# A two-layer encoder trunk in split-fp32 matmuls: the FFN in three parts, and the matmul operands moved to the front of SBUF

## The reference, cut to what matters

```python
for layer in range(2):
    h = rms_norm(x, mixer_norm_w[layer])
    if layer == 0:   # banded attention beside spatial gating, from ONE projection of 3584 columns
        mixed = concatenate([attn, sgu]) @ hyb_w_out
    else:            # stick-breaking attention, 16 heads of 128
        mixed = attention(h @ sb_w_qkv) @ sb_w_out
    x = x + mixed
    h = rms_norm(x, ffn_norm_w[layer])
    x = x + (silu(h @ w_gate[layer]) * (h @ w_up[layer])) @ w_down[layer]   # hidden width 5632
```

## Time and profile before

| what | value |
|---|---|
| median of the runs | 2164.94 us |
| the profiled execution, span | 2163.0 us |
| TensorE busy | 2156.0 us (100%) |
| VectorE busy | 1178.2 us (54%) |
| ScalarE busy | 988.2 us (46%) |
| read from HBM | 395.62 MB, mean 184 GB/s |
| granted TensorE clock in the slices | 9 tenths or more in all 40 |

### The profile page before, as it was taken

The page is one execution under the profiler, slowest core; times in us unless marked ns, Lnnn a source line. Parts: engine busy times, 40 slices in busy tenths (PEclk is TensorE's granted clock), DMA queues, the critical chain, the costliest instruction groups (busy, mean ns, idle before and its releaser), DMA issues.

```text
span 2163.0 us, 26223 instructions
## 1 busy us (share of the span) xinstructions
PE 2156.0 (100%) x9708; PEld 1769.2 (82%) x9708; DVE 1178.2 (54%) x1282; ACT 988.2 (46%) x1150; POOL 8.8 (0%) x19
## 2 busy tenths in 40 slices
PE   9999999999999999999999999999999999999999
PEld 8777888888888888888888888888888888888887
DVE  6777555555555544444565566555555555544443
ACT  6466554444444444444455445554444444443433
POOL 1000000000000000000000000000000000000000
PEclk9999999999999999999999999999999999999999
DMA  9544565565556545555545554556555655555553
GB/s 327 184 137 156 175 194 187 183 193 186 190 187 194 190 166 186 177 203 185 191 159 162 169 174 159 177 189 194 186 184 192 194 185 185 192 175 190 199 203 107
DMA packets 199154, 398.41 MB, mean 184 GB/s; under 512 B 6641, under 2 KB 6657, under 8 KB 198849
## 3 DMA queue, kind: packets, MB, share of 16 engines
q1 hardware_dynamic: 197728, 392.72, 55.3%
q0 software_dynamic: 960, 2.90, 0.4%
q10 hardware_dynamic: 416, 2.13, 0.3%
HBM read 395.62 MB, written 2.10 MB: 184 GB/s over the span
## 4 chain that ended last, share of the span: by engine, by line
PE 98%; ACT 1%; DVE 1%; DMA 0%; issue 0%; SPq 0%
PE acc L956 31%; PE acc L958 31%; PE acc L957 31%; PE turn L972 2%; PE turn L1042 0%; PE turn L1092 0%; PE zb L1067 0%; DVE w_lo L622 0%; PE zb L1027 0%; DMA raw<-in_w_in 0%; PE turn L1010 0%; PE zb L1068 0%; PE turn L1093 0%; ACT w_hi L418 0%; ACT att L526 0%; PE zb L1080 0%
## 5 line engine op out<-in xcount | busy, mean ns | idle before, releaser
L622 DVE TENSOR_TENSOR w_lo<-raw,w_hi 128x1024 fp32r<-128x1024 f32 (+1 forms) x760 | 906.6, 1201 | 697.5 <-ACT w_hi L418 696.2
L418 ACT ACTIVATE w_hi<-raw 128x1024 fp32r<-128x1024 f32 (+1 forms) x760 | 790.7, 1041 | 929.5 <-PE acc L958 926.3
L956 PE MATMUL acc<-w_hi,xT_hi 128*128 128x512 f32 x2016 | 793.5, 394 | 1.4 <-DVE w_lo L622 1.4
L958 PE MATMUL acc<-w_hi,xT_lo 128*128 128x512 f32 x2016 | 785.3, 390 | 0.0
L957 PE MATMUL acc<-w_lo,xT_hi 128*128 128x512 f32 x2016 | 785.0, 389 | 0.0
L956 PEld LDWEIGHTS acc<-w_hi,xT_hi 128*128 128x128 f32 x2016 | 378.6, 188 | 81.5 <-issue 4.8
L958 PEld LDWEIGHTS acc<-w_hi,xT_lo 128*128 128x128 f32 x2016 | 378.5, 188 | 79.1
L957 PEld LDWEIGHTS acc<-w_lo,xT_hi 128*128 128x128 f32 x2016 | 378.7, 188 | 78.1 <-issue 1.7
L956 PE MATMUL acc<-w_hi,hT_hi 128*128 128x512 f32 x704 | 279.5, 397 | 0.0
L958 PE MATMUL acc<-w_hi,hT_lo 128*128 128x512 f32 x704 | 279.1, 396 | 0.0
L957 PE MATMUL acc<-w_lo,hT_hi 128*128 128x512 f32 x704 | 279.0, 396 | 0.0
(11 more groups left out here) (151 smaller groups left out, 702.7 us busy)
## 6 DMA issues: line engine op xcount, KB each, us to landing
raw<-in_w_gate SPq DMA_DIRECT2D x88, 1024.0 KB, 5.1
raw<-in_w_up SPq DMA_DIRECT2D x88, 1024.0 KB, 5.1
raw<-in_w_down SPq DMA_DIRECT2D x80, 1024.0 KB, 5.0
raw<-in_w_qkv SPq DMA_DIRECT2D x48, 1024.0 KB, 5.1
raw<-in_w_out SPq DMA_DIRECT2D x32, 1024.0 KB, 5.0
raw<-in_w_in SPq DMA_DIRECT2D x26, 1024.0 KB, 5.2
raw<-in_w_down SPq DMA_DIRECT2D x16, 512.0 KB, 3.6
raw<-in_w_in SPq DMA_DIRECT2D x4, 512.0 KB, 6.9
```

Of the source, the lines that this page charges most:

```text
L418: nc.scalar.activation(w_hi[:, s % RING, 0:nk, :], raw[:, u % RING, k:k + nk, :], ACTF.Copy).then_inc(hi_ready, 1)
L622: nc.vector.tensor_tensor(w_lo[:, s % RING, 0:nk, :], raw[:, (s // 2) % RING, k:k + nk, :], f32(w_hi[:, s % RING, 0:nk, :]), ALU.subtract) ...
L956: nc.tensor.matmul(dst, h, wh, start=q == 0 and k == 0, stop=False)
L958: ins = nc.tensor.matmul(dst, l, wh, start=False, stop=q == ph.per_chunk - 1 and k == nk - 1)
```

## The change

It has two sides.

**Layout.** The declarations are put in another order: `xT_hi`, `xT_lo`, `w_hi`, `w_lo`, then one pair `m_hi`/`m_lo` of 16 k-tiles for both layers, then `x_sb`, `raw` and the constants. From the declared sizes, in KiB: `xT_hi` 0 to 16, `xT_lo` 16 to 32, `w_hi` 32 to 48, `w_lo` 48 to 64, `m_hi` 64 to 80, `m_lo` 80 to 96, `x_sb` 96 to 112, `raw` 112 to 144. `hT`, `m0` and `m1` are gone.

**Three parts.** The hidden width of the FFN, 11 blocks of 512, is made and multiplied in parts of 4, 4 and 3 blocks: up (4 iterations), down (4 iterations over these 16 k-tiles), up, down, up (3 iterations), down (12 k-tiles, in units of [4, 4, 2, 2]). The hidden activations of a part lie in `m_hi`/`m_lo`, where the mixer's result lay. Each down part adds its product to x. Parts 0 and 1 add in place in `x_sb`; only the last part of layer 0 makes the sum in `hid` and renews `xT`, as before. There are 16 phases in place of 8. The number of weight tiles, of main matmuls, of transposes and the bytes from HBM stay as they are.

```diff
-DOWN = [4] * 5 + [2, 2] + [4] * 5
+PARTS = [4, 4, 3]
+REST = [4, 4, 2, 2]
+FEED_FORWARD = [ph for n, part in enumerate(PARTS)
+                for ph in (("up", part, 2, FULL, n), ("down", D // CH, 1, FULL if part == 4 else REST, n))]
 PHASES = [
-    ("in", 1, 7, FULL), ("out", 4, 1, FULL), ("up", FFN // CH, 2, FULL), ("down", D // CH, 1, DOWN),
-    ("qkv", 4, 3, FULL), ("out", 4, 1, FULL), ("up", FFN // CH, 2, FULL), ("down", D // CH, 1, DOWN),
+    ("in", 1, 7, FULL, 0), ("out", 4, 1, FULL, 0), *FEED_FORWARD,
+    ("qkv", 4, 3, FULL, 0), ("out", 4, 1, FULL, 0), *FEED_FORWARD,
 ]
...
+        self.renews = self.name == "out" or self.name == "down" and self.part == len(PARTS) - 1 and n < len(PHASES) - 1
...
-        x_sb = sb("x_sb", [P, TT, D])
         xT_hi = sb("xT_hi", [P, KT, SEQ], F32R)
         xT_lo = sb("xT_lo", [P, KT, SEQ], F32R)
-        raw = sb("raw", [P, RING, 4, CH])
         w_hi = sb("w_hi", [P, RING, 2, CH], F32R)
         w_lo = sb("w_lo", [P, RING, 2, CH], F32R)
+        m_hi = sb("m_hi", [P, KT, SEQ], F32R)
+        m_lo = sb("m_lo", [P, KT, SEQ], F32R)
+        x_sb = sb("x_sb", [P, TT, D])
+        raw = sb("raw", [P, RING, 4, CH])
...
-            if ph.name == "out":
-                return (m0_hi, m0_lo) if ph.layer == 0 else (m1_hi, m1_lo)
-            return (hT_hi, hT_lo) if ph.name == "down" else (xT_hi, xT_lo)
+            return (m_hi, m_lo) if ph.name in ("out", "down") else (xT_hi, xT_lo)
...
-                    dve.wait_ge(kept, 1 + (D // CH) * before + (0 if row is None else i))
+                    if ph.renews:
+                        dve.wait_ge(kept, 1 + (D // CH) * ph.rows0 + i)
+                    else:
+                        dve.wait_ge(kept, 1 + (D // CH) * ph.rows0)
+                    if ph.name == "down" and ph.part:
+                        dve.wait_ge(x_added, 2 * ((before - 1) * (D // CH) + i) + 2)
...
+                elif not prev.turns:
+                    return
...
-                        pe.wait_ge(x_added, 2 * (RESIDUAL[n][0] * (D // CH) + i - 1) + tt + 1)
+                        pe.wait_ge(x_added, 2 * (ph.before * (D // CH) + i - 1) + tt + 1)
```

More of the change, by code:

```diff
@@ L61, with __init__ @@
 class Phase:
-    def __init__(self, n, unit0, chunk0, turn0):
-        self.name, self.count, self.chunks, self.unit_tiles = PHASES[n]
-        self.layer = 0 if n < 4 else 1
+    def __init__(self, n, unit0, chunk0, turn0, up0, before, rows0):
+        self.name, self.count, self.chunks, self.unit_tiles, self.part = PHASES[n]
+        self.layer = 0 if n < LAYER1 else 1
+        self.hidden0, self.up0 = sum(PARTS[:self.part]), up0
+        self.before, self.rows0 = before, rows0
+        self.renews = self.name == "out" or self.name == "down" and self.part == len(PARTS) - 1 and n < len(PHASES) - 1
         self.units = self.chunks * len(self.unit_tiles)
@@ L70, in __init__ @@
         self.unit0, self.half0, self.chunk0, self.turn0 = unit0, 2 * unit0, chunk0, turn0
-        self.turns = {"in": 23, "out": 1, "up": 1, "down": 1 if n < 7 else 0, "qkv": 4}[self.name]
+        self.turns = {"in": 23, "out": 1, "up": 1, "down": int(self.renews), "qkv": 4}[self.name]
     def half(self, i, s):
@@ L92, in make_phases @@
 def make_phases():
-    out, unit0, chunk0, turn0 = [], 0, 0, 0
+    out, unit0, chunk0, turn0, up0, before, rows0 = [], 0, 0, 0, 0, 0, 0
     for n in range(len(PHASES)):
-        ph = Phase(n, unit0, chunk0, turn0)
+        ph = Phase(n, unit0, chunk0, turn0, up0, before, rows0)
         out.append(ph)
@@ L100, in make_phases @@
         turn0 += ph.count * ph.turns
+        up0 += ph.count if ph.name == "up" else 0
+        before += ph.name in ("out", "down")
+        rows0 += ph.renews
     return out
@@ L148, with residual_of @@
 LOG_EXP_SET = 6
-RESIDUAL = {1: (0, 1, "ffn0"), 3: (1, 2, "mix1"), 5: (2, 3, "ffn1"), 7: (3, None, None)}
+RENEWALS = [(1, "ffn0"), (2, "mix1"), (3, "ffn1")]
+RESIDUALS = sum(ph.name in ("out", "down") for ph in PH)
+def residual_of(ph):
+    return (ph.before, *(RENEWALS[ph.rows0] if ph.renews else (None, None)))
 def diagonal(ap):
@@ L332, in unit @@
                     w, col = weights(ph, i, c)
-                    src = w.rearrange("(k p) n -> p k n", p=P)[:, k0:k0 + nk, bass.ds(col, CH)]
+                    row = (ph.hidden0 * GRP if ph.name == "down" else 0) + k0
+                    src = w.rearrange("(k p) n -> p k n", p=P)[:, row:row + nk, bass.ds(col, CH)]
                     if n == 0 and u in (0, 1):
@@ L439, in residual @@
             def residual(ph, i, t):
-                before, row, name = RESIDUAL[PH.index(ph)]
+                before, row, name = residual_of(ph)
                 if row is None:
@@ L533, in in_work @@
                         take_hi(ph.turn(0, IN_TURN[f"o{n}"]),
-                                [m0_hi[o * 64:o * 64 + 64, 2 * g:2 * g + 2, T * P:(T + 1) * P] for o in range(2)],
+                                [m_hi[o * 64:o * 64 + 64, 2 * g:2 * g + 2, T * P:(T + 1) * P] for o in range(2)],
                                 [o4[o * 64:o * 64 + 64, :, o, :] for o in range(2)])
@@ L979, in residual @@
             def residual(ph, i, t):
-                before, row, _ = RESIDUAL[PH.index(ph)]
+                before, row, _ = residual_of(ph)
                 if row is not None and t == ph.slots + 1:
```

47 lines of the change are left out of this document (21 added, 26 removed).

## The result

The changed kernel takes 2148.04 us (2147.97 to 2148.19, 4 runs), against 2164.94 us before. The ratio is 0.9923 with a 95% interval of 0.9908 to 0.9937. The forecast was 2149 us, faster. The number came out; the cause that it named, the place of the operands in SBUF, did not, as the experiments show. That the new order brought the gain all the same was luck.

A forecast was written before the change was run, and what follows sets the result against it. The prediction took TensorE's stream of matmuls, which hardly waits, to bound the kernel. 2163.0 - 21.6 (stationary operands) + 6.0 (stalls) gave 2147.4 us of span, with 1.9 around it 2149.3, said as 2149; range 2145 to 2172.

The forecast's parts named there:

- What bounds the kernel, and that only the pace counts: TensorE, busy 2156.0 of 2163.0 us, hardly waits; its stream counts in full, gains of other engines or queues for nothing.
- The two paces: Matmul starts 226.7 ns apart in "up" on xT, about 234.2 in "down" and "out", ascribed to the stationary operand's place.
- Stationary operands to the front: 2880 matmuls of out and down, operands moved to 64 to 96 KiB, gain 7.5 ns each: 21.6 us; bounds 0 and 21.6.
- Weights to the front: Moving w_hi and w_lo down to 32 to 64 KiB changes nothing: 0; the ends are 0 and 67 us of gain.
- The argument from L1081: L1081, both operands far, is followed after 0.18 us, the far pace, so the moving operand's place has nothing to explain.
- More phases and iterations: Borders of the added phases and "down" iterations cost 0, since adds come in time; 2.4 us if cover fails.
- The stalls: Half-size units ending the last FFN part delay the add: 7 stalls of 0.85 us, 6.0 us; bounds 0.5 and 1.5 each.
- Around the span: 1.9 us added to get from the profiled execution, 2163.0 us, to the median of the runs, 2164.94.
- A: Rival: m at 64 to 96 KiB gains nothing, only the stalls remain: 2170.9 us, or 2168.5 with small stalls; 13 in 100.
- B: Rival: step between 64 and 96 KiB, m_lo stays far, gain 14.4 us in place of 21.6: 2156.5 us; 6 in 100.
- C: Rival: the weights' near place pays too, 7.5 ns on each of 8928 matmuls, another 67 us: 2082 us; 13 in 100.
- D: Rival: stationary operand and weights in one region disturb each other; 6048 matmuls lose 7.5 ns: 2194.7 us; 6 in 100.

The follow-up runs named there:

- layout_only: The kernel before with only the layout changed (xT and weights first, then m or hT; x_sb, raw, constants at the top of SBUF), without the three parts: 2143.11 us.
- both_far: The changed kernel with xT and the weights w_hi and w_lo moved to the top of SBUF, m at 16.1 to 48.1 KiB: 2166.13 us.
- consts_top: The kernel before with the constants and small buffers at the top of SBUF, so m and hT begin 3,936 bytes lower: 2143.10 us.
- m_shifted: The changed kernel with 96 unused bytes in front of m_hi: 2168.16 us.
- small_mid: The changed kernel with the units of the last FFN part in the order [4, 2, 2, 4] in place of [4, 4, 2, 2]: 2143.72 us.
- parts_only: The changed kernel with the tensors in the order of the kernel before, m behind the constants at 131.8 to 163.8 KiB: 2168.54 us.

## Why the prediction was right, and where it was wrong

*What bounds the kernel, and that only the pace counts.* Right. The phases of the table above account for the gain within 0.2 us.

*The two paces.* Right as a reading: 226.7 and 234.2 ns, by the stationary operand, with the pair of accumulators excluded. **The failed step is the next sentence: "What remains different is the place of the stationary operand, and it acts like a step."** The flatness over 88 KiB of `hT`, which I read as the far side of a step, fitted just as well that the distance doesn't matter at all: what `m` and `hT` had in common was their low address bits. layout_only has no step where one had to be, both_far has a fast pair at the top of SBUF, and consts_top and m_shifted turn the pace over with 3,936 and with 96 bytes. That "the step lies somewhere between 48 and 115.7 KiB" was thus a bound on something that isn't there. The declared sizes, from which I worked out the places, held the hint: I rounded the constants to "some 3.7" KiB, and they are 3,812 bytes as declared and 3,936 as they lie, neither a multiple of 256.

*Stationary operands to the front, -21.6 us.* The size is right: 2880 matmuls by 7.5 ns, and layout_only and consts_top measure 21.7 to 21.8 without any stall. The reason is that in the new order `m` follows the weights directly, and all sizes up to there are multiples of 16 KiB, so that all three start alike. For this term the prediction was right by luck.

*Weights to the front, 0.* Right. The argument from L1081 proved nothing: from the declared sizes, `tri_r` minus `soft_lo` is 160 modulo 256 in the kernel before, an offset that is slow in the table above. The mean distance from L1081 to the matmul behind it is 174 to 177 ns in every run. None of them brought these two to the same alignment, so that its slow pace has the same origin is likely, but not shown.

*More phases and iterations, 0.* Right: in the timeline of the changed kernel the distances between starts at the borders of iterations in "up" and `out` are the pace itself, and a longer one, by 0.45 to 0.55 us, stands only at the 7 borders of part 2.

*The stalls, +6.0 us.* The mechanism and the count were right, and small_mid shows both; the size was too large: 0.56 us each and not 0.85, 3.9 us in all, and small_mid gave 4.3 back. The estimate added three durations in full. In the timeline above the add starts 0.29 us ahead of E and not 0.1, the second add follows the first after 0.60 us and not 0.69, and TensorE starts 0.14 us after that and not 0.25.

*Around the span, 1.9 us.* It was 1.8.

So 2163.0 - 21.6 + 6.0 + 1.9 was off by 1.3 us. The stalls were 2.1 us too large; against that stand `out`, which gained 5.3 and not 5.8, and 0.2 in in and qkv. The small rest lies outside these stretches.

*The rivals.* A, B, C and D were all built on place, with different borders; none of them is what happens. A would have been the result if `m` had followed the constants, as parts_only shows (2168.54 against the 2168.5 to 2170.9 of A), so the 13 in 100 stood for a real danger under a wrong name. D's picture, that two operands disturb each other depending on where each lies, was nearest to what the runs show, but it went by large regions, where the runs show the starts modulo 256 bytes. What I should have said is that the sign hung on an accident of allocation.

*The rules of the Trainium skill.* The warm distance that the Trainium skill gives for single matmuls (TensorE: Matmul & The Clock Gate, section Back-to-back issue gap), by which I estimated 215.8 ns for 512 columns, was met as a lasting pace at no offset tried; the best is 226.7. The same page of the Trainium skill (section Step-by-step: what each phase is for) says that loading the next stationary operand takes no read bandwidth from the running matmul. The runs show something next to it: the pace of matmuls with their loads depends on where the two operands start relative to each other, 226.7 to 234.2 ns. No run separates the load from the matmul, so whether the two meet at the same memory is not shown.

## What to carry to other kernels

When TensorE never waits, read the distance between the starts of equal matmuls phase by phase; if two phases differ, compare the start addresses of their operands, and first the low bits. In this kernel the stationary and the moving fp32r operands want starts that are equal modulo 256 bytes, wherever they were put: keep small odd-sized buffers out of the line between them, or pad to 256. If starts can't be equal, mind the direction: 64 bytes one way and 64 the other are not the same offset. Before a program is rebuilt to fit a layout, try the layout alone: here it was worth 21.7 us without the rebuilding, and the rebuilding cost 3.7 to 4.9. And where an accumulator is reused at once, end its iteration with full-size work, so that taking the result out of PSUM has cover.

## What the runs showed of the hardware that was not expected

- The pace of fp32r matmuls of 512 columns, each with its own load of 128 stationary columns, is 226.7 ns if both operands start alike modulo 256 bytes and 232.4 to 234.2 ns at offsets of 64, 96, 128 and 160 (stationary minus moving). The absolute place had no effect in the layouts tried: with equal starts the pace was 226.7 ns with the stationary operand at 16 to 48, 80 to 168, 128 to 216 and 192 to 224 KiB. Offsets within one tensor by multiples of 512 bytes (position tiles, k-tiles) have none either.
- Halves at changing offsets carry something over: behind a misaligned half, an aligned one needs several matmuls to come to its pace (236.8 to 226.8 ns over eleven distances at offset 256). Halves whose weights begin 64 bytes beyond `xT`, between others at 32 and 96, settle at 228.9 ns instead, in a pattern of three distances.
- Why it is 256 bytes, why the loss is 5.7 to 7.5 ns, and what the last 13 ns above 213.3 (an estimate, 512 columns at one per cycle of 2.4 GHz) are, is open. Offsets of 32, 192 and 224 bytes stood in mixed halves only. Offsets below 32 bytes were not tried, nor other widths of the moving operand.
